# Two heads at a time on two halves of the TensorE array, and a 64-byte pad: a two-block transformer kernel

## What is computed

```python
# sliding window branch (SWA): 16 query heads, 4 key/value heads, window 128
scores = einsum('bnqkgd,bnskd->bnkgqs', qb, kb) * HEAD_DIM ** -0.5   # a block of 128 queries, 256 keys
probs = softmax(concatenate([where(mask, scores, -inf), sink], -1), -1)[..., :-1]
out = einsum('bnkgqs,bnskd->bnqkgd', probs, vb) * silu(z)

# forgetting branch (FOX): 16 heads with keys and values of their own
sc = einsum('bqhd,bkhd->bhqk', q_block, k[:, :end]) * scale
sc = sc + cum[:, :, start:end, None] - cum[:, :, None, :end]         # sums of log sigmoid(f)
out = einsum('bhqk,bkhd->bqhd', softmax(where(causal, sc, -inf)), v[:, :end]) * silu(z)
```

## Time and profile before

| | |
|---|---|
| median of 3 runs | 3832.13 us (3831.87 to 3833.36) |
| the profiled execution's own time | 3828.45 us |
| its span, first to last instruction | 3826.7 us |
| mean granted TensorE clock | 0.979 |
| TensorE busy | 3628.0 us (95%) |
| GpSimd, VectorE, ScalarE busy | 2161.6, 1494.1, 802.3 us |
| output records L699 | 159.5 us, 1088 of them |
| transposes L691 | 93.1 us, 544 |

### The profile page before, as it was taken

How to read it: one execution, slowest core, us unless ns; L and a number is a source line. 1 busy time by engine, 2 the same in 40 slices (tenths; PEclk the granted TensorE clock), 3 DMA queues, 4 the chain that set the end, 5 groups by cost and what they waited for, 6 DMA issues and landing times.

```text
span 3826.7 us, 49528 instructions
## 1 busy us (share of the span) xinstructions
PE 3628.0 (95%) x17270; PEld 2882.9 (75%) x17270; DVE 1494.1 (39%) x2756; ACT 802.3 (21%) x1585; POOL 2161.6 (56%) x2116
## 2 busy tenths in 40 slices
PE   7999899999999899989999999999899999999998
PEld 6777688877777688867877777777678777777776
DVE  4555421114455322036744442222366545422223
ACT  1123111001222111012214422221122134222211
POOL 6745467667554577665655554435655564544445
PEclk9999999999999999989999999999999999999999
DMA  3211122222111122222122111111221121211111
GB/s 122 84 60 66 66 77 99 94 93 77 67 66 55 67 98 99 99 88 77 66 77 77 66 66 57 64 55 66 79 84 70 67 79 64 77 66 55 56 65 66
DMA packets 39871, 284.60 MB, mean 74 GB/s; under 512 B 4688, under 2 KB 5200, under 8 KB 5728
## 3 DMA queue, kind: packets, MB, share of 16 engines
q1 hardware_dynamic: 38880, 282.13, 20.5%
q10 hardware_dynamic: 896, 1.14, 0.1%
HBM read 281.15 MB, written 2.10 MB: 74 GB/s over the span
## 4 chain that ended last, share of the span: by engine, by line
PE 82%; DVE 10%; issue 4%; ACT 3%; POOL 1%; DMA 0%; DVEq 0%; ACTq 0%; POOLq 0%
PE banks L302 19%; PE banks L304 19%; PE banks L303 19%; PE banks L699 4%; PE banks L792 2%; PE banks L517 2%; PE banks L519 2%; PE banks L518 2%; PE banks L691 2%; PE banks L794 1%; PE banks L347 1%; PE banks L346 1%; PE banks L345 1%; PE banks L488 1%; PE banks L754 1%
## 5 line engine op out<-in xcount | busy, mean ns | idle before, releaser
L265 POOL TENSOR_SCALAR whi<-raw 128x512 fp32r<-128x512 f32 x1056 | 736.8, 707 | 1628.5 <-PE banks L304 1427.9
L270 POOL TENSOR_TENSOR wlo<-raw,whi 128x512 fp32r<-128x512 f32 x1056 | 1470.4, 1403 | 0.0
L302 PE MATMUL banks<-xhi,whi 128*128 128x512 f32 x2976 | 1206.8, 406 | 36.4 <-DVE xlo L1127 15.3
L304 PE MATMUL banks<-xhi,wlo 128*128 128x512 f32 x2976 | 1166.8, 392 | 0.0
L303 PE MATMUL banks<-xlo,whi 128*128 128x512 f32 x2976 | 1165.9, 392 | 0.0
L302 PEld LDWEIGHTS banks<-xhi,whi 128*128 128x128 f32 x2976 | 562.7, 189 | 196.9 <-issue 51.3
L304 PEld LDWEIGHTS banks<-xhi,wlo 128*128 128x128 f32 x2976 | 562.5, 189 | 121.7
L303 PEld LDWEIGHTS banks<-xlo,whi 128*128 128x128 f32 x2976 | 563.9, 189 | 114.6 <-issue 6.7
L302 PE MATMUL banks<-yhi,whi 128*128 128x512 f32 x544 | 218.7, 402 | 17.2 <-DVE ylo L1290 5.6
L1558 DVE CUSTOM_DVE_ANT_0 banks<-banks,wide_mask 128x128 f32<-128x128 f32 (+3 forms) x128 | 63.9, 500 | 395.5 <-PE banks L794 395.5
L304 PE MATMUL banks<-yhi,wlo 128*128 128x512 f32 x544 | 215.9, 397 | 0.0
(11 more groups left out here) (232 smaller groups left out, 4190.2 us busy)
## 6 DMA issues: line engine op xcount, KB each, us to landing
raw<-weights SPq DMA_DIRECT2D x264, 1024.0 KB, 4.8
x<-x_in SPq DMA_DIRECT2D x1, 2048.0 KB, 8.1
out<-merged SPq DMA_DIRECT2D x1, 2048.0 KB, 6.3
rot<-const SPq DMA_DIRECT2D x1, 512.0 KB, 11.8
rot<-const ACTq DMA_DIRECT2D x1, 512.0 KB, 3.3
wide_mask<-const ACTq DMA_DIRECT2D x1, 384.0 KB, 4.0
wide_mask<-const SPq DMA_DIRECT2D x1, 256.0 KB, 12.5
cst<-const SPq DMA_DIRECT2D x1, 232.0 KB, 8.3
```

The source lines that it names most:

```text
L265: pool.tensor_scalar(whi[p][:, w], raw[p][:, w], 1.0, 1.0, ALU.mult, ALU.mult).then_inc(s("hi_written"), 1)
L270: return pool.tensor_tensor(wlo[p][:, w], raw[p][:, w], whi[p][:, w].bitcast(F32), ALU.subtract)
L302: pe.matmul(dst, whi[p][:, w], hi[:, k, :], start=start and i == 0, stop=False)
L304: mm = pe.matmul(dst, wlo[p][:, w], hi[:, k, :], start=False, stop=stop and last_k)
```

## The change

Units are counted differently (`head_block`): units 2m and 2m + 1 are now an even and an odd head on the same block. TensorE's loop goes over pairs. The scores of both heads are issued in turn, matmul by matmul, the one in the upper and the other in the lower 64 rows of the array; in FOX the two decay rows follow. The outputs of both heads alternate in the same way, in the two halves of the array's columns, and there is one count of `outputs` for a pair. The order is scores of pair m + 1, fill, turn 2m, outputs of pair m - 1, turn 2m + 1. Two units are scored ahead in place of three. `pt2` has four buffers in place of two; `pr2` still has two. ScalarE copies turn u - 2 behind exp u (it was u - 1), and the tanh of z stands before the last two copies. VectorE divides u before it takes the maximum of u + 2. The fills are shared out anew: (4, 4, 3, 1) in SWA and (2, 1, 1, 1, 2, 1, 2, 1) in FOX, with four and five steps ahead of the loop (it was four and three). `nsink` grows from 16 to 32 numbers, which moves all that lies behind it by 64 bytes, and `work` from 4 to 6 tiles; the launch reserves 1024 bytes for dynamic DMA.

```diff
--- before.py
+++ after.py
@@ -67,6 +67,12 @@
+def head_block(u, units):
+    c, k = divmod(u, units // 2)
+    return 2 * c + k % 2, k // 2
...
@@ -130,7 +136,7 @@
         wide_mask = sb("wide_mask", [P, C_C1 - C_WM2])
-        nsink = sb("nsink", [P, 16])
+        nsink = sb("nsink", [P, 32])
...
@@ -187,8 +193,8 @@
         v2 = sb("v2", [P, QB, 256], F32, t4)
-        work = sb("work", [P, 4, S], F32, t4)
-        rotated, kv, pr2, pt2 = work[:, 0:3, :], work[:, 3, :], work[:, 0:2, :], work[:, 2:4, :]
+        work = sb("work", [P, 6, S], F32, t4)
+        rotated, kv, pr2, pt2 = work[:, 0:3, :], work[:, 3, :], work[:, 0:2, :], work[:, 2:6, :]
...
@@ -681,43 +687,52 @@
-                def attend(name, it, n, units, score, keys, blocks, values, fills):
+                def attend(name, it, n, units, score_pair, keys, blocks, values, fills):
...
                             pe.wait_ge(s(name + "_pt"), units * it + u)
-                        for j in keys(u):
+                        for j in keys(head_block(u, units)[1]):
...
-                    def output(u):
-                        pe.wait_ge(s(name + "_pt"), units * it + u + 1)
-                        for r, b, js in blocks(u):
-                            o = 64 * (r % 2)
+                    def output_pair(m):
+                        pe.wait_ge(s(name + "_pt"), units * it + 2 * m + 2)
+                        r, block = head_block(2 * m, units)
+                        for b, js in blocks(block):
                             for i, (v, j) in enumerate(js):
-                                mm = pe.matmul(psum[o:o + 64, r // 2, b * P:(b + 1) * P], values(r, v),
-                                               pt2[:, u % 2, j * P:(j + 1) * P], start=i == 0, stop=i == len(js) - 1)
+                                for h in range(2):
+                                    mm = pe.matmul(psum[64 * h:64 * h + 64, r // 2, b * P:(b + 1) * P], values(r + h, v),
+                                                   pt2[:, (2 * m + h) % 4, j * P:(j + 1) * P],
+                                                   start=i == 0, stop=i == len(js) - 1)
...
-                    for u in range(3):
-                        score(u)
+                    def scores_of(m):
+                        if m:
+                            pe.wait_ge(s(name + "_probs"), units * it + 2 * m - 1)
+                        score_pair(m)
+                    scores_of(0)
...
                     fill(2 * KT - sum(fills))
-                    for u in range(units):
-                        if u + 3 < units:
-                            score(u + 3)
-                        if fills[u]:
-                            mm = fill(fills[u])
-                            if not sum(fills[u + 1:]):
+                    for m in range(units // 2):
+                        if m + 1 < units // 2:
+                            scores_of(m + 1)
+                        if fills[m]:
+                            mm = fill(fills[m])
+                            if not sum(fills[m + 1:]):
                                 mm.then_inc(wave_done, 1)
-                        turn(u)
-                        if u:
-                            output(u - 1)
-                    output(units - 1)
+                        turn(2 * m)
+                        if m:
+                            output_pair(m - 1)
+                        turn(2 * m + 1)
+                    output_pair(units // 2 - 1)
...
@@ -742,28 +757,26 @@
-                    def score(u):
-                        r, hf = divmod(u, 2)
-                        if u >= 3:
-                            pe.wait_ge(s("swa_probs"), 8 * it + u - 2)
-                        dst = 4 + u % 3
-                        o = 64 * (r % 2)
+                    def score_pair(m):
+                        r, hf = head_block(2 * m, 8)
...
                             k0 = max(blk - 1, 0) * P
-                            mm = pe.matmul(psum[:, dst, b * 256 + (0 if blk else P):(b + 1) * 256],
-                                           q2[o:o + 64, r // 2, blk * P:(blk + 1) * P],
-                                           q2[o:o + 64, 2, k0:(blk + 1) * P], start=True, stop=True)
-                        mm.then_inc(s("swa_scores"), 1)
-                    def blocks(u):
-                        r, hf = divmod(u, 2)
+                            for h in range(2):
+                                o = 64 * h
+                                mm = pe.matmul(psum[:, 4 + (2 * m + h) % 3, b * 256 + (0 if blk else P):(b + 1) * 256],
+                                               q2[o:o + 64, r // 2, blk * P:(blk + 1) * P],
+                                               q2[o:o + 64, 2, k0:(blk + 1) * P], start=True, stop=True)
+                                if b:
+                                    mm.then_inc(s("swa_scores"), 1)
+                    def blocks(hf):
...
                             blk = 2 * hf + b
-                            yield r, blk, [(blk - 1 + a, 2 * b + a) for a in range(2) if blk - 1 + a >= 0]
-                    attend("swa", it, n + 3, 8, score, lambda u: range(1 - u % 2, 4), blocks,
-                           lambda r, v: v2[:, v, 0:64], (1, 1, 2, 2, 2, 2, 2, 0))
+                            yield blk, [(blk - 1 + a, 2 * b + a) for a in range(2) if blk - 1 + a >= 0]
+                    attend("swa", it, n + 3, 8, score_pair, lambda hf: range(0 if hf else 1, 4), blocks,
+                           lambda r, v: v2[:, v, 0:64], (4, 4, 3, 1))
...
@@ -784,20 +797,20 @@
-                    def score(u):
-                        r, i = divmod(u, QB)
-                        if u >= 3:
-                            pe.wait_ge(s("fox_probs"), 16 * it + u - 2)
-                        dst, o, w = 4 + u % 3, 64 * (r % 2), (i + 1) * P
-                        pe.matmul(psum[:, dst, 0:w], q2[o:o + 64, r // 2, i * P:w], q2[o:o + 64, 2 + r // 2, 0:w],
-                                  start=True, stop=False)
-                        pe.matmul(psum[:, dst, 0:w], sel[:, r, :], cum[:, 1, 0:w], start=False, stop=True)\
-                          .then_inc(s("fox_scores"), 1)
-                    attend("fox", it, n + 3, 16, score, lambda u: range(u % QB + 1),
-                           lambda u: [(u // QB, u % QB, [(j, j) for j in range(u % QB + 1)])],
-                           lambda r, v: v2[:, v, r * 64:(r + 1) * 64],
-                           (1, 1, 0, 0, 1, 1, 1, 0, 1, 1, 1, 0, 2, 2, 1, 0))
+                    def score_pair(m):
+                        r, i = head_block(2 * m, 16)
+                        w = (i + 1) * P
+                        for h in range(2):
+                            o = 64 * h
+                            pe.matmul(psum[:, 4 + (2 * m + h) % 3, 0:w], q2[o:o + 64, r // 2, i * P:w],
+                                      q2[o:o + 64, 2 + r // 2, 0:w], start=True, stop=False)
+                        for h in range(2):
+                            pe.matmul(psum[:, 4 + (2 * m + h) % 3, 0:w], sel[:, r + h, :], cum[:, 1, 0:w],
+                                      start=False, stop=True).then_inc(s("fox_scores"), 1)
+                    attend("fox", it, n + 3, 16, score_pair, lambda i: range(i + 1),
+                           lambda i: [(i, [(j, j) for j in range(i + 1)])],
+                           lambda r, v: v2[:, v, r * 64:(r + 1) * 64], (2, 1, 1, 1, 2, 1, 2, 1))
...
@@ -990,18 +1003,18 @@
                         act.wait_ge(s(name + "_turned"), units * it + u + 1)
-                        if u >= 2:
-                            act.wait_ge(s(name + "_outputs"), units * it + u - 1)
-                        turned = slice(P if name == "swa" and u % 2 == 0 else 0, parts(u)[-1][1])
-                        act.activation(pt2[:, u % 2, turned], psum[:, 7, turned], ACT.Copy).then_inc(s(name + "_pt"), 1)
+                        if u >= 4:
+                            act.wait_ge(s(name + "_outputs"), units // 2 * it + u // 2 - 1)
+                        lo, hi = parts(head_block(u, units)[1])
+                        act.activation(pt2[:, u % 4, lo:hi], psum[:, 7, lo:hi], ACT.Copy).then_inc(s(name + "_pt"), 1)
...
                             act.wait_ge(s(name + "_turned"), units * it + u - 1)
-                        for i, (lo, hi) in enumerate(parts(u)):
+                        lo, hi = parts(head_block(u, units)[1])
+                        for i, (lo, hi) in enumerate([(lo, 256), (256, hi)] if name == "swa" else [(lo, hi)]):
...
@@ -1009,17 +1022,16 @@
                             act.activation(st2[:, 3, 2 * u:2 * u + 2], st2[:, 1, 2 * u:2 * u + 2], ACT.Exp,
-                                           bias=sinks(u // 2)).then_inc(s("swa_part"), 1)
+                                           bias=sinks(head_block(u, units)[0])).then_inc(s("swa_part"), 1)
...
                             ins.then_inc(s(name + "_probs"), 1)
-                        if u == units - 1:
-                            act.wait_ge(wave_done, z + 1)
```

(21 more changed lines are left out.)

8 lines of the change are left out of this document (3 added, 5 removed).

## The result

The changed kernel takes 3797.41 us (median, 3796.94 to 3808.93), the kernel before 3832.74 us on the same chip: a ratio of 0.9914, 95% interval 0.9895 to 0.9933. That is 35 us less; the prediction said 56. The gain is a little over a third smaller than forecast; the sign and the wide range (3745 to 3810) hold, while the forecast's own range of 3750 to 3797 is missed by 0.4.

A forecast was written before the change was run, and what follows sets the result against it. TensorE was taken to bound the attention stages. Stages -55.2, pad -5.8 and clock +5.4 make -55.6 us from the profiled 3828.45, or 3776.5 after adding 3.7 for the median; own range 3750 to 3797, wide range 3745 to 3810.

The forecast's parts named there:

- Two halves run side by side: Paired scores and outputs: the second head's time vanishes, TensorE's work falling 11.8 us per FOX group, 7.0 per SWA group.
- The waits that come instead: TensorE's turns wait for exp and copy on ScalarE: net +6.3 us per FOX group, +5.6 per SWA group.
- FOX -5.5 a group: Forgetting-branch stages: net +6.3 us of waits against -11.8 of TensorE work, windows near 39.5.
- SWA -1.4: Sliding-window stages, per group: net +5.6 us of waits against -7.0 of TensorE work, windows near 30.4.
- The clock: TensorE's clock falls in four of eight SWA stages instead of two, after longer waits at turn 1: +5.4 us.
- The pad: Branch and FFN products speed up to 0.680 us a triple once on 128-byte multiples: -5.8 us, else 0.
- columns did overlap: Denies the rival that column halves do not overlap when single matmuls alternate in outputs: +31 us, 3807, chance 0.12.
- strict order: Rival: matmuls start and end in order, so head 1's scores start with head 0's last record: 3800, chance 0.05.
- halves do not drain: Denies the rival that every change of half drains the array, so no stream overlaps: 3842 to 3927, chance 0.04.
- the second rival: The clock falls in most attention stages: +32 us, 3808, chance 0.16.

The follow-up runs named there:

- e4: The changed kernel with ScalarE copying turn u - 2 ahead of exp u, not behind it: 3753.16 us, ratio 0.9797.
- e5: The changed kernel with two of SWA's 16 filling steps moved from ahead of turn 0 to between turns 0 and 1: 3781.21 us, ratio 0.9874.
- e1: The changed kernel without its pad, `nsink` back at 16 numbers: 3788.21 us, ratio 0.9888.
- e3: The changed kernel with `nsink` at 64 numbers, a pad of 192 bytes in place of 64: 3785.07 us, ratio 0.9878.
- e6: The changed kernel with a pair's outputs issued one head after the other, not alternating: 3803.80 us, ratio 0.9935.
- e7: e3 with 128 bytes more put ahead of x, so operand and weight buffers start on 256-byte multiples: 3782.51 us, ratio 0.9874.
- e9: e8 with one filling step moved between turns 0 and 1 and one between a group's last two turns: 3766.21 us, ratio 0.9838.
- e8: e4 with `nsink` at 64 numbers, the pad of e3: 3744.64 us, ratio 0.9778.
- e11: e8 with only one filling step moved from ahead of the loop to between turns 0 and 1, in SWA and FOX: 3730.85 us, ratio 0.9734.

## Why the prediction was right, and where it was off

- *Two halves run side by side*: right. Twelve paired output records in 0.88 and the FOX window show it. In FOX TensorE's busy time fell from 44.36 to 33.05, 11.3 us a group (forecast 11.8), in SWA from 30.16 to 23.40, 6.8 (forecast 7.0).
- *The waits that come instead*: right in place, cause and nearly in size. The SWA rows read 2.06, 1.25, 1.12, 1.42 and 0.69 where 2.1, 1.2, 1.0, 1.5 and 0.9 were written. Window less busy rose by 5.8 in FOX (forecast 6.3) and by 5.9 in SWA (forecast 5.6). e4 shows the cause for about half of them, which go with the copy ahead of the exponential. One step of the working does not follow from its words: SWA's net of +5.6 is the 7.5 less nearly all of today's 1.8, while the text lets only 1.09 of it go, which would give +6.4. The trace bears the number out and not the words: 1.65 us of idle time in a group before, 7.59 after.
- *FOX -5.5 a group*: 39.5 forecast, 39.49 measured. This carried the sign. *SWA -1.4*: 0.8 measured (30.99 for 30.4), 5 us in all on the wrong side, the sum of two misses of 0.3 us a group in a small difference of large terms.
- *The clock*: right in sum (+5.4 forecast, +5.8 read as 7 x 1.6 less 2 x 2.7), by two errors that cancel, and so by luck. It fell in seven groups, not four, and each fall cost 1.6, not 2.7, because it lasted half as long, 3.41 us in place of 6.83; TensorE was busy throughout either. Why it is shorter is open. That the long wait at turn 1 draws the lower clock is what e5 shows: cover the wait, and no fall is left behind turn 1. How often it does so is partly chance: with the same wait in e1, e3, e6 and e7 it fell there in three, six, seven and five groups of eight, so a count of falls read from one execution is worth a few us either way.
- *The pad*: the step that failed. It was forecast at -5.8, with 0 as the only other value, and measured at (544 x 0.0105 + 352 x 0.0135) = +10.5 in the triples; e1, without it, came out 9.2 lower, on another chip. The error was to read "x starts on a 128-byte multiple and is quick, y does not and is slow" as a cause. The rows fitted as well to "x starts level with its weights" (which the later runs bear out as a rule of thumb, though not as the cause), and the prediction named no row against that; its sentence that a loss was not excluded should have given a bound on that side. This step alone is 16 of the 21 us by which the forecast was low; SWA's windows are the other 5.
- *Rivals*: columns did overlap (e6 bounds how far ahead a half can start), strict order does not hold, halves do not drain. The clock fell in most SWA groups, as the second rival had it, but in no FOX window, and cheaply, so its +32 did not come.

By pieces: FOX -44.4, SWA -0.8, pad +10.5, together -34.7, against -35.3 in the medians. The pieces are read from two profiled executions, though, and these differ by 31.5 only (3828.45 and 3796.94). Some 3 us more lie outside the windows and triples; the mean granted clock is 0.974 after and 0.979 before, which may be where, but that is not shown.

## What to carry to other kernels

When two halves of the array are paired, TensorE's work shrinks and the next thing in line is the engine that feeds it: look at what stands in that engine's queue ahead of the short step that TensorE waits for, and reorder that before anything else (here 44 us from one moved copy, more than the change itself gave). Put independent matmuls into the gaps that remain, above all into a long first one, but first ask which later step waits for the last of them, and look at the clock behind every wait that is left: in e9 it cost more than the waits themselves. And of an address that seems to matter, ask "relative to what": change it alone, in both directions, before trusting it.

## What the runs showed of the hardware that was not expected

- Where its buffers start changes the price of a 512-column float32 product: three in 0.680, 0.687 or 0.697 to 0.699 us, as the operand starts 0, 64 or 128 bytes from the weights modulo 256 (rows above and the earlier trace rows). Moving everything together by 128 bytes changes nothing (e7). Why is open, and so is whether the distance to the weights is what counts: an address modulo 512 fits too, and six records whose two operands kept their distance went from 1.077 to 1.080 with the pad. Distances of 192 and other sizes next to the weights were not tried.
- A matmul for one half of the array starts ahead of earlier ones for the other half, by about three records and not more in these output rows (e6). Where each head has four records the order of issue made no difference (0.66 either way), beyond that they must alternate.
- One wait of 2.06 us early in a stage went with a fall of the clock right behind it in 28 of 40 groups of five kernels (after, e1, e3, e6, e7); with 1.36 us of it covered, in none of eight (e5). In e4, e8 and e11 falls come at the end of a group instead, where three waits of about 1.1, 1.0 and 0.7 us follow each other; they differ from group to group with the same code, so their exact condition stays open.
